# Decode reads that add up in one PSUM bank through zero-padded query columns

## The reference, cut to what matters

```python
S = S * s_dec + jnp.einsum('bshk,bshv->bhkv', k_dec, vb)   # one state (key x value) per token and head
o = jnp.einsum('bthk,bhkv->bthv', q_dec, S)                # the decode read: 8 tokens, 8 states
o_gla = (rms_norm(o_gla, gla_norm_w) * jax.nn.silu(heads(g_out, GLA_HEADS))).reshape(bsz, L, GLA_VAL)
yz = y.reshape(bsz, L, SSD_INNER) * jax.nn.silu(z)         # the state-space group is normed later
```

## Time and profile before

| | |
|---|---|
| median of 3 runs | 1032.12 us (1032.03 to 1035.11) |
| the profiled execution's own time | 1031.38 us |
| its span, first to last instruction | 1029.7 us |
| TensorE busy (matmul) | 977.8 us, 95% of the span |
| VectorE, ScalarE, GpSimd busy | 388.3, 277.0, 107.9 us |
| mean granted TensorE clock | 0.986 |

### The profile page before, as it was taken

The page is one execution under the profiler, slowest core; times in us unless marked ns, Lnnn a source line. Parts: engine busy times, 40 slices in busy tenths (PEclk is TensorE's granted clock), DMA queues, the critical chain, the costliest instruction groups (busy, mean ns, idle before and its releaser), DMA issues.

```text
span 1029.7 us, 12780 instructions
## 1 busy us (share of the span) xinstructions
PE 977.8 (95%) x5031; PEld 631.6 (61%) x5031; DVE 388.3 (38%) x936; ACT 277.0 (27%) x591; POOL 107.9 (10%) x177
## 2 busy tenths in 40 slices
PE   8999999899989999999997998999989999999995
PEld 6777777688866454545444876777866354545443
DVE  2467786773025021212113335665235021212114
ACT  4534434223023110000002166777123100100002
POOL 2322224161000000000000001112200000000000
PEclk9999999899998999999999999999999999999999
DMA  9933536947751999999999343332692999999991
GB/s 386 356 156 123 210 138 229 394 178 297 285 194 33 424 411 424 421 420 422 422 422 427 145 164 121 138 130 87 254 374 89 423 413 423 420 422 421 422 378 44
DMA packets 39183, 299.65 MB, mean 291 GB/s; under 512 B 5000, under 2 KB 6536, under 8 KB 8648
## 3 DMA queue, kind: packets, MB, share of 16 engines
q1 hardware_dynamic: 33696, 268.52, 64.1%
q0 software_dynamic: 4928, 29.72, 7.8%
q10 hardware_dynamic: 496, 0.53, 0.1%
HBM read 283.32 MB, written 15.53 MB: 290 GB/s over the span
## 4 chain that ended last, share of the span: by engine, by line
PE 76%; ACT 8%; DVE 7%; DMA 6%; issue 2%; POOL 1%; ACTq 0%; DVEq 0%; POOLq 0%
PE bank L1182 20%; PE bank L1206 10%; PE bank L827 9%; PE bank L1076 6%; PE bank L1218 5%; PE bank L1167 5%; PE bank L1330 4%; PE bank L1096 2%; PE bank L1343 2%; DMA ring<-in_w_up 2%; ACT ring L1515 2%; PE bank L1110 1%; PE bank L1104 1%; DMA spread<-v_rows 1%; DMA W<-in_conv_cols 1%
## 5 line engine op out<-in xcount | busy, mean ns | idle before, releaser
L1182 PE MATMUL bank<-ring,A 128*64 128x512 f32 x880 | 223.0, 592 | 2.3 <-issue 1.7
L827 PE MATMUL bank<-xT,ring 128*128 128x264 f32 x704 | 165.0, 390 | 2.7 <-ACT A L1428 1.4
L827 PEld LDWEIGHTS bank<-xT,ring 128*128 128x128 f32 x704 | 132.0, 191 | 32.7 <-issue 9.3
L1182 PEld LDWEIGHTS bank<-ring,A 128*64 128x64 f32 x880 | 73.8, 137 | 123.9 <-issue 123.9
L1206 PE MATMUL bank<-ring,W 128*64 128x512 f32 x448 | 113.4, 595 | 0.9 <-ACT W L1658 0.9
L2223 DVE TENSOR_TENSOR W<-W,bank 128x512 f32<-128x512 f32 x16 | 11.0, 688 | 203.6 <-PE bank L1182 203.6
L1343 PE MATMUL bank<-xT,ring 128*128 128x264 f32 x320 | 80.0, 395 | 0.0
L1206 PEld LDWEIGHTS bank<-ring,W 128*64 128x64 f32 x448 | 34.9, 137 | 60.9 <-issue 59.8
L754 POOL TENSOR_SCALAR xT<-xT,vecs 128x264 f32<-128x264 f32 x4 | 5.6, 1396 | 604.3 <-DVE xT L2077 604.3
L1343 PEld LDWEIGHTS bank<-xT,ring 128*128 128x128 f32 x320 | 58.4, 192 | 11.0 <-issue 1.8
L1218 PE MATMUL bank<-W,A 128*128 128x264 f32 x256 | 63.5, 392 | 1.7 <-issue 1.7
(11 more groups left out here) (310 smaller groups left out, 1180.5 us busy)
## 6 DMA issues: line engine op xcount, KB each, us to landing
ring<-in_w_gate SPq DMA_DIRECT2D x56, 1024.0 KB, 13.2
ring<-in_w_down SPq DMA_DIRECT2D x56, 1024.0 KB, 13.4
ring<-in_w_up SPq DMA_DIRECT2D x54, 1024.0 KB, 16.2
ring<-in_w_ab SPq DMA_DIRECT2D x10, 2048.0 KB, 8.2
ring<-in_w_c SPq DMA_DIRECT2D x8, 2048.0 KB, 13.7
A<-in_w_up SPq DMA_DIRECT2D x10, 1024.0 KB, 13.9
ring<-in_w_oab SPq DMA_DIRECT2D x4, 2048.0 KB, 9.2
A<-in_w_gate SPq DMA_DIRECT2D x8, 1024.0 KB, 12.8
```

The lines of the kernel that those rows point to most:

```text
L827: mm = pe.matmul(ab_bank(m)[:, 0:T], slot(AB_IN0 + m // 4, 8)[:, c, (m % 4) * P:(m % 4 + 1) * P], xT[:, c, :], start=(c == 0), stop=(c == ...
L1182: mm = pe.matmul(bank[i][64 * j:64 * j + 64, :], xg[:, 2 * (pair % 2) + j, c, :], slot(n0 + 6 * pair + 2 * i + j, 8)[:, c, :], start=(c == ...
```

## The change

The four reads of a half keep their quarters, but both halves write the **same** `dv` columns and add up. That works since a token's query column no longer fills 32 columns: it stands alone in a block of 32 that is zero elsewhere, in column 0 for the first half (token q) and in column 1 for the second (token 4+q). `padded_query` is that block; `query_columns` is where VectorE writes the 8 live columns. GpSimd clears the blocks once per layer for the heads, VectorE once for the groups (`s_cz`).

So what is behind a read halves: one square of `dv` columns, one sum, one scaling. The turn is now a transpose of 128x128 per 128 columns (`J` of them, 4 for a group) in place of the matmuls against `every32`, and its result, 128 columns wide, goes to bank 6 (bank 2 for the last head of layer 0, bank 4 for the last of layer 1, bank 7 for a group). VectorE picks the 8 columns 32q and 32q+1 out of it.

Waits change with the banks. `turn_out` also waits until ScalarE has copied the next head's decode values out of bank 6. The wait for `heads_reads_placed` moves from `scores` to `turn_v`, which writes bank 6. In a group both reads come first, then the fill; the turn waits for `ssd_prompt_state`. The second output portion (`out_part(1)`, bank 7) waits for `ssd_outputs_read`. `spread_eg(0)` moves on GpSimd's queue from the first stage to behind `spread_x(0)`, as its target lay where the padded columns are now.

```diff
+        def query_columns(h):
+            at = 5632 + 256 * (h % 2)
+            return W[:, at:at + 258].rearrange("p (i x) -> p i x", x=129)[:, :, 0:P:32]
+        def padded_query(h, b):
+            at = 5632 + 256 * (h % 2) + 32 * b
+            return W[:, at:at + 32]
...
-            spread_eg(0)
             pool.wait_ge(sem("heads_out_ready"), 3)
...
             spread_x(0)
+            spread_eg(0)
...
@@ turn_v, scores
+                    if h >= 3:
+                        pe.wait_ge(sem("heads_reads_placed"), n - 2)
...
-                    if h >= 2:
-                        pe.wait_ge(sem("heads_reads_placed"), n - 1)
...
@@ outputs
-                            mm = pe.matmul(bank[3][32 * q:32 * q + 32, i * dv:(i + 1) * dv],
-                                           QS[:, h % 2, b:b + 1].to_broadcast([P, 32]), decode_state(layer, h, b),
-                                           start=True, stop=True)
+                            mm = pe.matmul(bank[3][32 * q:32 * q + 32, 0:dv],
+                                           padded_query(h, b), decode_state(layer, h, b),
+                                           start=(i == 0), stop=(i == 1))
...
@@ turn_out
-                    for i in range(NB // 4):
-                        for j in range(J):
-                            mm = pe.matmul(read_turned(layer, J)[:, j * NB + 4 * i:j * NB + 4 * i + 4],
-                                           READ[:, i * dv + j * P:i * dv + (j + 1) * P], every32, start=True, stop=True)
-                    mm.then_inc(sem("heads_reads_turned"), 1)
+                    pe.wait_ge(sem("heads_kv_copied"), 3 * min(n + 2, H0 + nh - 1) + 2)
+                    for j in range(J):
+                        tr = pe.transpose(read_turned(H0 + h, J)[:, j * P:(j + 1) * P], READ[:, j * P:(j + 1) * P], ident[:, :])
+                    tr.then_inc(sem("heads_reads_turned"), 1)
...
@@ state-space groups
                 reads(0)
+                reads(1)
                 feed(4)
                 pe.wait_ge(sem("ssd_prompt_state"), g + 1)
-                reads(1)
-                for i in range(2):
-                    pe.wait_ge(sem("ssd_reads_copied"), 2 * g + i + 1)
-                    for j in range(4):
-                        mm = pe.matmul(bank[4][:, 256 + j * NB + 4 * i:260 + j * NB + 4 * i],
-                                       s_read[:, i, j * P:(j + 1) * P], every32, start=True, stop=True)
-                mm.then_inc(sem("ssd_state_used"), 1)
+                pe.wait_ge(sem("ssd_reads_copied"), g + 1)
+                for j in range(4):
+                    tr = pe.transpose(bank[7][:, j * P:(j + 1) * P], s_read[:, j * P:(j + 1) * P], ident[:, :])
+                tr.then_inc(sem("ssd_state_used"), 1)
...
@@ squares (ScalarE), scaled (VectorE)
-                    act.activation(READ[:, 0:2 * dv], bank[3][:, 0:2 * dv], ACT.Square, scale=dv ** -0.5).then_inc(
+                    act.activation(READ[:, 0:dv], bank[3][:, 0:dv], ACT.Square, scale=dv ** -0.5).then_inc(
...
-                    for i in range(2):
-                        st.add(dve.tensor_scalar(READ[:, i * dv:(i + 1) * dv], bank[3][:, i * dv:(i + 1) * dv],
-                                                 hms[:, h % 2, 2 + i:3 + i], None, ALU.mult))
+                    st.add(dve.tensor_scalar(READ[:, 0:dv], bank[3][:, 0:dv], hms[:, h % 2, 2:3], None, ALU.mult))
```

More of the change, by code:

```diff
@@ L500, in score_bank, with read_turned @@
             return bank[4 if layer else 2]
-        def read_turned(layer, J):
-            return bank[4][:, 256:256 + J * NB] if layer else bank[2][:, 400:400 + J * NB]
+        def read_turned(n, J):
+            return bank[{3: 2, 11: 4}.get(n, 6)][:, 256:256 + J * P]
         def x_spread(b):
@@ L526, in trunk_program @@
         XB_LATE = area(7168, 2, 512)
-        s_read = area(8320, 2, 512)
+        s_read = area(8320, 512)
+        s_cz = W[:, 8832:9088]
+        s_cz_columns = W[:, 8832:9090].rearrange("p (i x) -> p i x", x=129)[:, :, 0:P:32]
         s_sq = area(9344, 4, T)
@@ L763, in _ @@
             stage_end(pool, 4)
-            st.run(pool.memset(SC_BLOCKS, 0.0))
+            st.add(pool.memset(SC_BLOCKS, 0.0))
+            st.add(pool.memset(W[:, 5632:6144], 0.0))
+            st.settle()
             pool.sem_inc(sem("scores_cleared"), 1)
@@ L1050, in reads @@
                         b = 4 * i + q
-                        mm = pe.matmul(bank[5 + 2 * i][32 * q:32 * q + 32, :], CT[:, NP + b:NP + b + 1].to_broadcast([P, 32]),
-                                       ssd_state(g, b).rearrange("p h v -> p (h v)"), start=True, stop=True)
-                    mm.then_inc(sem("ssd_reads_ready"), 1)
+                        mm = pe.matmul(bank[5][32 * q:32 * q + 32, :], s_cz[:, 32 * b:32 * b + 32],
+                                       ssd_state(g, b).rearrange("p h v -> p (h v)"), start=(i == 0), stop=(i == 1))
+                    if i == 1:
+                        mm.then_inc(sem("ssd_reads_ready"), 1)
                 pe.wait_ge(sem("ssd_dec_updated"), 2 * g + 2)
                 reads(0)
+                reads(1)
                 feed(4)
                 pe.wait_ge(sem("ssd_prompt_state"), g + 1)
-                reads(1)
-                for i in range(2):
-                    pe.wait_ge(sem("ssd_reads_copied"), 2 * g + i + 1)
-                    for j in range(4):
-                        mm = pe.matmul(bank[4][:, 256 + j * NB + 4 * i:260 + j * NB + 4 * i],
-                                       s_read[:, i, j * P:(j + 1) * P], every32, start=True, stop=True)
-                mm.then_inc(sem("ssd_state_used"), 1)
+                pe.wait_ge(sem("ssd_reads_copied"), g + 1)
+                for j in range(4):
+                    tr = pe.transpose(bank[7][:, j * P:(j + 1) * P], s_read[:, j * P:(j + 1) * P], ident[:, :])
+                tr.then_inc(sem("ssd_state_used"), 1)
             ab_copied(pe, AB_CHUNKS - 1)
@@ L1497, in roots @@
                     act.wait_ge(sem("heads_sums"), n + 1)
-                    st.run(act.activation(hms[:, h % 2, :], hms[:, h % 2, :], ACT.Ln, bias=eps_col[:, :]))
-                    act.activation(hms[:, h % 2, :], hms[:, h % 2, :], ACT.Exp, scale=-0.5).then_inc(sem("heads_roots"), 1)
+                    st.run(act.activation(hms[:, h % 2, 0:3], hms[:, h % 2, 0:3], ACT.Ln, bias=eps_col[:, :]))
+                    act.activation(hms[:, h % 2, 0:3], hms[:, h % 2, 0:3], ACT.Exp, scale=-0.5).then_inc(sem("heads_roots"), 1)
                 def place_out(h):
@@ L1586, in _ @@
                 act.sem_inc(sem("ssd_state0"), 1)
-                for i in range(2):
-                    act.wait_ge(sem("ssd_reads_ready"), 2 * g + i + 1)
-                    act.copy(s_read[:, i, :], bank[5 + 2 * i][:, :]).then_inc(sem("ssd_reads_copied"), 1)
-                    if i == 0:
-                        take_ab(m0 + 5)
+                act.wait_ge(sem("ssd_reads_ready"), g + 1)
+                act.copy(s_read[:, :], bank[5][:, :]).then_inc(sem("ssd_reads_copied"), 1)
+                take_ab(m0 + 5)
                 act.wait_ge(sem("ssd_outputs_read"), 2 * g + 2)
@@ L1840, in queries @@
                 def queries(h):
-                    st.run(dve.tensor_scalar(QS[:, h % 2, :], qa(h)[:, NP:T], scale, None, ALU.mult))
+                    st.run(dve.tensor_scalar(query_columns(h), qa(h)[:, NP:T].rearrange("p (i q) -> p i q", i=2), scale, None, ALU.mult))
                     dve.sem_inc(sem("heads_queries"), 1)
@@ L1888, in sums @@
                         dve.wait_ge(sem("heads_squared"), 2 * n + i + 1)
-                        red = dve.tensor_reduce(hms[:, h % 2, 2 * i:2 * i + 2],
-                                                squares[:, 0:2 * dv].rearrange("p (i v) -> p i v", v=dv), AX, ALU.add)
+                        red = dve.tensor_reduce(hms[:, h % 2, 2 * i:2 * i + 2 - i],
+                                                squares[:, 0:(2 - i) * dv].rearrange("p (i v) -> p i v", v=dv), AX, ALU.add)
                         st.add(red)
@@ L1909, in place_reads @@
                     dve.wait_ge(sem("heads_reads_turned"), H0 + h + 1)
-                    dve.tensor_copy(oa(h)[:, :, NP:T], read_turned(layer, J).rearrange("p (j b) -> p j b", j=J)).then_inc(
-                        sem("heads_reads_placed"), 1)
+                    for j in range(J):
+                        put = dve.tensor_copy(oa(h)[:, j, NP:T].rearrange("p (i q) -> p q i", i=2),
+                                              read_turned(H0 + h, J)[:, j * P:(j + 1) * P].rearrange("p (q r) -> p q r", q=4)[:, :, 0:2])
+                    put.then_inc(sem("heads_reads_placed"), 1)
                 prep(0)
@@ L1964, in _ @@
                 h8 = lambda t: t.rearrange("p (h v) -> p h v", h=8)
+                if g == 0:
+                    st.run(dve.memset(s_cz, 0.0))
+                dve.wait_ge(sem("conv_silu"), CONV.index(C0 + g) + 1)
```

(1 more changed line is left out.)

14 lines of the change are left out of this document (7 added, 7 removed).

## The result

The kernel after takes 1028.96 us (median of 20 runs, 1023.16 to 1032.4) beside 1034.07 us for the kernel before (20 runs, 1029.03 to 1039.58): ratio **0.9944**, 95% interval 0.9923 to 0.9965. That is 5.1 us gained in these medians, 5.8 by the ratio; the forecast was 11.2, and its range (to 1024.5) does not hold the time. About 2 us of the distance lie outside the change: the kernel before stood at 1034.07 in these runs, 1.95 above the 1032.12 from which the forecast was taken. Even a range moved by that much would end at 1026.5. The single profiled execution after took 1024.45 us (span 1022.6), well under its own median. Single executions of either kernel lie within 11 us of each other, so from here on times are taken from medians and single executions serve to see where time goes.

A forecast was written before the change was run, and what follows sets the result against it. TensorE, busy 95% of the span, was taken as the bound, so its savings shorten the run nearly one for one. Terms 1.8 + 2.7 + 4.0 + 1.0 + 1.7 = 11.2 us gave 1020.9 us, range 1018.5 to 1024.5.

The forecast's parts named there:

- The turns, layers 0 and 1 and the groups: TensorE's transposes replacing 4-column matmuls, 0.11 us each: a turn saves 0.59 in layer 0, 1.37 per group, 0.36 in layer 1.
- Rival B: Turn transposes cost 0.22 us each, so turns save 5.0 in place of 7.4 us: 1023.3 us; chance 0.12.
- Six heads of layer 1: Second head stage: turn 0.36, scaling 0.26 and squares 0.05 save 0.67 us a head, 4.0 us in all.
- Rival C: Layer 1's loop is held elsewhere, such as by the next head's value spread; half of 5.0 us goes: 1023.4; chance 0.12.
- D: Slower: `turn_out`'s new wait hangs on ScalarE's copy and the previous head's store; 1035.5 us, chance 0.02.
- Layer 0: First head stage: two transposes per turn save 0.59 us, three heads on the path, 1.8 us; the fourth saves nothing.
- a group: ... both on the path: State-space stage: four transposes take 0.44 us and save 1.37 per group, both groups counting, 2.7 us.
- The sum: Whole kernel: 1.8 + 2.7 + 4.0 + 1.0 + 1.7 = 11.2 us gained.
- With ... less of thin work ahead of the 0.86, I expect the clock to stay up: Start of group 1: less 4-column matmul work ahead of 0.86 us idle avoids the clock fall, 1.7 us, least certain term.
- Rival A: The clock falls all the same in group 1, or once more elsewhere: 1022.6 us; chance 0.25.

The follow-up runs named there:

- the two kernels with all loads held: Kernel before and kernel after, each with all four output-projection weight loads held until group 1's spread of x landed: 1031.51 us and 1022.02 us.
- the groups alone with all loads held: Kernel before with only the state-space groups' part of the change, all four output-projection weight loads held until group 1's x spread landed: 1027.13 us, ratio 0.9944.
- the kernel with the turns four times over: Kernel after, second to fourth output-projection loads held until group 1's x spread landed, every transpose of a turn issued four times: 1026.48 us, ratio 0.9923.
- the same hold: Output-projection weight loads wait for group 1's x spread, on kernels before and after; second to fourth loads: 1030.88, 1022.41 us; all four: 1031.51, 1022.02 us.
- third set: Runs with the second to fourth output-projection loads held until group 1's x spread landed: kernel before 1030.88 us, kernel after 1022.41 us.
- second set: Runs including all four output-projection loads held until group 1's x spread landed: kernel before 1031.51 us, kernel after 1022.02 us.
- the heads alone: Kernel before with only the heads' part of the change, the groups' reads, turn and waits as before: 1027.34 us, ratio 0.9961.
- the heads alone with the hold: Kernel before with only the heads' part of the change, second to fourth output-projection loads held until group 1's x spread landed: 1027.27 us, ratio 0.9931.
- the groups alone: Kernel before with only the state-space groups' part of the change, the heads as before: 1032.25 us, ratio 1.0005.
- its second run: The kernel after, run once more with no edit: 1027.8 us, ratio 0.9946.

## Why the prediction was wrong, point by point

**The turns, layers 0 and 1 and the groups: right.** 0.22 us in layer 0, 0.16 in layer 1 (forecast 0.11), and 0.11 us a transpose in the groups. In the groups, the two kernels with all loads held compare cleanly, since the clock falls at the same place in both: 71.7 us before, 69.1 after. That is 2.6 us; the forecast had 2.7. The closeness owes something to the pair: the groups alone with all loads held, the same programs there, took 70.6 us, as the clock fell once more at their start (0.79 from 160 to 168 us, 1.00 in the two). Rival B (twice the price) falls.

**Six heads of layer 1: right.** From the first turn to the sixth the period was 14.41 us before ((705.95 - 633.89) / 5) and is 13.79 after ((697.95 - 628.99) / 5): 0.62 less, forecast 0.67. The whole stage is 5.0 us shorter (157.8 to 152.8), as forecast. Rival C (held elsewhere) falls, and so does D: no wait for ScalarE's copy shows at the turn. (D's time adds up to 1035.2, not 1035.5; nothing hangs on it.)

**Layer 0: right in its size, not in every execution.** Group 0 began at 159.2 to 160.1 us in six of nine executions with the new heads, at 161.6 to 162.1 in the five with the old ones: about 2 us, forecast 1.8. In the other three it began at 161.9 to 162.4. One of these is the kernel with the turns four times over, whose 18 transposes more in the first three turns are worth 2.0 us; why the other two were late is open.

**"a group: ... both on the path": the step that failed.** It looked at the turn's own surroundings in the earlier trace rows and went no further. Of the DMA line in the earlier trace rows it asked only what lies ahead of the expert stages, and concluded that an earlier TensorE moves everything behind it. Group 1's score products need `x` spread, and that runs on its own clock: the store leaves when VectorE has group 1's `x`, and then two transfers share the DMA queues with weights. The slack was 3.95 us. The forecast itself took 1.8 + 1.37 + 1.7 = 4.9 us off TensorE ahead of that point, so 0.9 us of wait was due by its own numbers, with the spread as early as before. In fact it came later too, since loads of SP's queue met the store and the broadcast. The 2.72 us of wait and the 1.6 us of slower rows behind it (below) are together 4.3 us; the two terms for the groups and the clock had promised 2.7 + 1.7 = 4.4, and the groups came out 0.1 us shorter. The Trainium skill, "DMA: Bandwidth & Descriptors", "Queues, rings and completion order", says that a DMA engine goes round the queues it has work for, packet by packet. The trace agrees. From 194.5 to 202 us after (packets, MB, share; q1 is SP's queue with the loads, q0 GpSimd's):

```profile
q1 hardware_dynamic: 143, 2.10, 67.6%
q0 software_dynamic: 127, 1.03, 33.2%
```

Packets of the two queues ran in nearly equal numbers. Taken alone, that rule would let 16 KB slip in between the loads; but the store has its own queue's broadcasts ahead of it, 1.25 MB, the first of which landed at 203.6 us (191.1 + 12.5), 3.5 us after the store was issued. What part of the last 2 us is the store's data and what part the report that they have landed, no run here separates.

**The sum: nearly right once that wait is gone.** With the same hold on both sides the change is worth 1022.41 / 1030.88 = 0.992, or 8.5 us (third set), and 1022.02 / 1031.51 = 0.991, or 9.5 us (second set). The sum without its clock term was 9.5. By the intervals of its two ratios each of the two differences is uncertain by nearly 5 us either way. They agree with 9.5, but would with 11.2 as well; the stages in the traces say more.

**"With ... less of thin work ahead of the 0.86, I expect the clock to stay up": not shown.** Windows over the start of group 1 in two kernels, the heads alone and the heads alone with the hold, both with the thin turns of 4 columns (the clock is the third figure from the end):

```profile
199.00:208.00 9.00, 8.95 (x50) 7.89 (x51) 8.06 (x20) 2.84 (x6) 3.10 (x6) 1.00 0.69 276
```

```profile
199.00:208.00 9.00, 8.14 (x41) 7.14 (x41) 7.67 (x19) 1.80 (x4) 3.93 (x7) 0.81 0.67 256
```

It stayed up in the first and fell in the second. Over all executions it fell there in 2 of 5 kernels with thin turns and in none of 9 with transposes. That leans towards the forecast, yet 2 in 5 is not a fall each time: on average it is worth 0.7 us (an estimate, 2/5 of 1.7), not 1.7. The prediction took what one profile showed for what happens every time. Rival A, and the rule of the Trainium skill that stands beside it ("TensorE: Matmul & The Clock Gate", Part 4, that transposes do not count as busy), would have it fall after too. It did not in those nine, one of which has four times as many transposes.

**The new wait cost clock as well.** The window over the score products of group 1, after and in the groups alone:

```profile
222.00:234.00 12.00, 9.82 (x70) 6.48 (x70) 8.26 (x15) 1.18 (x3) 0.80 (x1) 0.86 0.00 0
```

```profile
222.00:234.00 12.00, 7.08 (x58) 5.17 (x58) 10.11 (x13) 0.00 (x0) 4.72 (x5) 0.72 0.00 0
```

In all four kernels with a wait of 2.7 to 5.1 us there, the clock was 0.72 to 0.86 in this window, a mean that holds a stretch at 0.50, the lower level of 1.2 GHz; in the ten without the wait it was 1.00. So 2.72 us of waiting cost the kernel after another 1.6 us in the next two rows alone (2.83 in place of 1.97, and 1.90 in place of 1.13). A wait of that length is not always followed by a fall: ahead of the same products in group 0 all 14 kernels wait 2.3 to 3.7 us, and in two of them (2.31 and 3.20 us) the products behind it ran at full clock.

**What the sum did not have: a part given back behind layer 1.** The heads show 5 to 7 us in the traces up to the second norm and 4.0 to 4.2 in the medians (0.9961; 0.9972 to 0.9931). From that norm to the second experts it is 25.8 to 26.2 us in the five kernels with the old heads, 27.3 to 28.0 in seven of the nine with the new ones and 26.3 in the other two. The rows that differ most are the products that gather tokens for the experts, before and after:

```profile
781.51 6.32 PE L1167 MATMUL bank<-A,W 128*128 128x224 f32 x32 [0.32 <-DVEq L2172]
```

```profile
772.67 7.13 PE L1180 MATMUL bank<-A,W 128*128 128x224 f32 x32
```

The granted clock around them is 1.00 before (781.0 to 788.7 us) and 0.86 after (772.0 to 780.6). From norm to experts the new heads lose 1.4 us on average, which brings traces and medians together within the intervals. Why the clock falls there more often with the new heads stays open.

## What to carry to other kernels

When an edit makes the busiest engine earlier, go down its list to every point where it meets the others and write down two times: when it came there, and when what it needs was ready. The smallest difference is what the edit can give, as long as it doesn't move the operands themselves; here it was 3.95 us, read from one row of VectorE. Then ask which loads the earlier progress will set free: a prefetch that isn't wanted for 20 us can slow a 16 KB store on which all waits, and whatever stands ahead of that store on its own queue. Holding the prefetch back by two waits was worth as much as the change itself.

## What the runs showed of the hardware

The size of what bulk loads do to a small transfer was not expected: the same 16 KB store took 1.8 to 3.3 us from issue to landing where at most one load of 2 MB had gone out ahead of it, and 3.6 to 9.4 where two had.

The spread between executions comes in good part from the granted clock around waits of TensorE. The norm behind the first experts, after and in its second run:

```profile
554.44 3.83 PE L1123 MATMUL bank<-A,ones 128*128 128x264 f32 x16 [3.31 <-ACT A L1618]
```

```profile
559.11 6.86 PE L1123 MATMUL bank<-A,ones 128*128 128x264 f32 x16 [3.28 <-ACT A L1618]
```

The same matmuls behind the same wait took 3.83 us at full clock and 6.86 where the clock was 0.70 in the mean from 560 to 580 us, of which these matmuls fill the first six. The stage in which they lie took 277.2 us in the first execution and 283.3 in the second: as large a difference as the change makes. Over the 20 executions of the kernel after, the four with a mean granted clock of 0.981 or less took 1030.3 to 1032.4 us, the four with 0.988 or more 1024.8 to 1029.7.
